# Weaving the samples' window attention into the latent stage, with another order of the recurrence levels

## The chip, the cores and the metric

The kernel runs on one core of a Trainium2 chip (trn2). The metric is the device time of one launch in microseconds (us). The kernel before takes 1953.93 us, the median of three runs (1951.99 to 1957.06).

## The reference

One inference step of a decoder trunk of two layers. A prompt of 256 tokens and eight samples of one token each (264 columns, `NT`) go through it together. A layer is

```
x += 1/2 * SwiGLU_1(RMSNorm(x))
x += W_out [ A | B | C | D ](RMSNorm(x) @ W_in)
x += 1/2 * SwiGLU_2(RMSNorm(x))
A: latent attention; for a sample over 16 pages of 128 cached latents, which are
   multiplied by w_uk and normalised before the scores, then softmax and context
B: causal dilated window attention, patterns (128,1), (512,4), (2048,16); for a sample
   the keys and values come from cache_swa_k / cache_swa_v by stride: 3 x 128 rows of 256
C: mLSTM matrix memory            D: HGRN2 gated linear recurrence, chunkwise
```

For the samples, C and D are one step of a stored state. All is float32.

## The kernel before, in words

Activations stay in SBUF, transposed (`x_T`, `h_T`: 128 x 8 x 264). All weights stream through a ring of three slots (`ring`) by DMAs that SP issues. TensorE, VectorE, ScalarE, GpSimd (called PE, DVE, ACT and POOL in the rows) and SP each run a list written out by hand, joined by semaphores. The order of work on an engine is thus the order of the calls in its loop over the layers, and an instruction that waits holds up all that stands behind it on its engine. A layer has these stages:

1. Feed-forward 1.
2. **Mixing**: the projection by `W_in` in 34 pieces (`project` on TensorE, `copy_out` on ScalarE, through two PSUM banks), and between the pieces the prompt's parts of A, B, C and D. D is computed in eight `level`s of block size 128 to 1. For a level GpSimd subtracts decays (`level_decays`, into `D1v`), ScalarE takes exponentials (`level_exp`, into `E1v`), VectorE multiplies (`level`), TensorE makes the scores (`level`), and VectorE masks them into `ATD` (`level_mask`). `hgrn` on TensorE multiplies them by the values, turns the gates of the samples and the end keys and makes the end state. Then `HCD` is normalised and turned into `o_T`.
3. **Latent stage** (`latent_samples`, on all engines): for each of the eight samples 16 pages, in pairs. TensorE turns and multiplies pages, ScalarE squares and copies, VectorE sums. A sample's scores need a maximum over all partitions. VectorE leaves `latent_max` in the next sample's time, GpSimd computes `partition_all_reduce`, and VectorE takes it up in `latent_shift` one sample later still. Between these reductions GpSimd also updates the stored states of C and D (`state_d_decay`, `state_d_products`, `state_c_decay`, `state_c_products`, after samples 2, 3, 4 and 5).
4. **Tail**: TensorE's `samples` spreads the queries over the partitions, VectorE's `states` finishes C and D, and `windows` does B: for each sample a tile of keys (`KB`, two slots, loaded by SP) is multiplied by the query (`Qbc`) and summed. Then come a maximum on GpSimd, exponentials, a sum, probabilities, the product with the values (`VB`, loaded by GpSimd's queue after the last context) and the addition into `o_T` (`mixer_done`).
5. `w_out`, then feed-forward 2.

In `latent_samples`, `b` is the sample, `g` the page and `c` a group of four pages. `settled` only moves a semaphore on.

## Time and profile before

| | |
|---|---|
| median of 3 runs | 1953.93 us |
| the profiled execution's own time | 1961.99 us |
| its span | 1960.4 us |
| TensorE matmuls busy | 1677.5 us (86%) |
| VectorE busy | 769.1 us (39%) |
| ScalarE busy | 325.7 us (17%) |
| GpSimd busy | 235.5 us (12%) |
| mean granted TensorE clock | 0.913 of full speed |

The 1.6 us between span and time lie around the program. Times in the rows count from the start of the span. In the first layer mixing runs from 270 to 515 us, the latent stage from 515 to 662, the tail from 662 to 709, `w_out` to 740. The second layer repeats this some 967 us later. In a row of the timeline the bracket tells how long the engine had been idle and what ended that; "issue" means that nothing the profile shows did. The share of busy time says little here: both feed-forward parts keep TensorE full, and the time that can go lies in the three stages between them.

### The profile page before, as it was taken

The numbers are of one execution on the slowest core, as the hardware profiler recorded it, in microseconds if no ns is written. First come the engines' busy times: TensorE is split into PE (matmuls) and PEld (weight loads), VectorE is DVE, ScalarE is ACT, GpSimd is POOL, SyncE is SP. The second block draws the span as 40 slices with busy tenths as digits, with TensorE's granted clock in tenths as the row PEclk, the third lists the DMA queues.
The fourth block names the chain that finished last, engine by engine and source line by source line (L and its number), as shares of the span: only waits on it lengthen the run. The fifth ranks groups of instructions, "written<-read, shape, count | busy, mean of one in ns | idle before, by whom it ended". The sixth has DMA issues, their size and how long they took to land.

```text
span 1960.4 us, 25417 instructions
## 1 busy us (share of the span) xinstructions
PE 1677.5 (86%) x8942; PEld 1354.5 (69%) x8942; DVE 769.1 (39%) x1403; ACT 325.7 (17%) x854; POOL 235.5 (12%) x307
## 2 busy tenths in 40 slices
PE   4999989976878368999979999899767863799998
PEld 3888867655666157888858888576665651688887
DVE  3444114653456343442124431175434645334411
ACT  1000002421545100000000000033224531000000
POOL 2000001222312310000000000012222322100000
PEclk9999999987789579999989999999777985899999
DMA  6875533320701437786548855232124024568742
GB/s 211 300 255 189 148 107 122 98 66 7 222 2 33 154 110 232 245 291 169 165 154 272 274 161 153 86 126 70 47 93 137 2 87 129 161 203 275 256 129 81
DMA packets 232153, 295.15 MB, mean 151 GB/s; under 512 B 10264, under 2 KB 215240, under 8 KB 228328
## 3 DMA queue, kind: packets, MB, share of 16 engines
q1 hardware_dynamic: 221128, 191.63, 32.2%
q0 software_dynamic: 10912, 102.08, 15.2%
q8 instruction: 62, 1.02, 0.2%
q14 instruction: 51, 0.42, 0.1%
HBM read 287.43 MB, written 73.33 MB: 184 GB/s over the span
## 4 chain that ended last, share of the span: by engine, by line
PE 75%; issue 10%; DVE 5%; POOL 2%; POOLq 2%; DVEq 1%; ACT 1%; DMA 1%; SPq 0%; ACTq 0%
PE bank L1632 32%; PE bank L1649 16%; PE bank L1670 8%; PE bank L1994 3%; PE bank L1676 3%; PE bank L1824 2%; POOLq L604 2%; PE bank L1606 2%; PE bank L1930 2%; DMA h_T<-in_cache_swa_k 1%; PE bank L1666 1%; DVE h_T L1044 1%; PE bank L1949 1%; PE bank L1872 1%; PE bank L1975 1%
## 5 line engine op out<-in xcount | busy, mean ns | idle before, releaser
L1632 PE MATMUL bank<-h_T,ring 128*128 128x264 f32 x2816 | 636.0, 390 | 27.9 <-DVE h_T L1044 27.9
L1632 PEld LDWEIGHTS bank<-h_T,ring 128*128 128x128 f32 x2816 | 540.6, 192 | 123.7 <-issue 29.9
L1649 PE MATMUL bank<-act_T,ring 128*128 128x264 f32 x1408 | 313.9, 386 | 0.0
L1649 PEld LDWEIGHTS bank<-act_T,ring 128*128 128x128 f32 x1408 | 267.5, 190 | 45.8
L1670 PE MATMUL bank<-ring,h_T 128*128 128x256 f32 (+2 forms) x512 | 162.9, 476 | 9.2 <-DVE h_T L1044 9.2
L1051 DVE TENSOR_SCALAR sg<-sg 128x264 f32<-128x264 f32 x88 | 26.2, 298 | 363.8 <-ACT sg L683 363.8
L1053 DVE RECIPROCAL sg<-sg 128x264 f32<-128x264 f32 x88 | 158.6, 1803 | 6.5
L1930 PE MATMUL bank<-wuk,TM 128*128 128x288 f32 x512 | 148.5, 437 | 0.0
L1670 PEld LDWEIGHTS bank<-ring,h_T 128*128 128x128 f32 x512 | 102.2, 204 | 62.1 <-issue 52.6
L1064 DVE SCALAR_TENSOR_TENSOR x_T<-bank,x_T 128x264 f32<-128x264 f32 x48 | 20.7, 432 | 301.3 <-PE bank L1649 259.4
L683 ACT ACTIVATE sg<-bank 128x264 f32<-128x264 f32 x88 | 34.3, 390 | 627.3 <-PE bank L1632 627.3
L1412 DVE TENSOR_REDUCE decs<-TM 128x8 f32<-128x512 f32 x128 | 87.3, 685 | 89.9 <-ACT TM L949 88.2
L1930 PEld LDWEIGHTS bank<-wuk,TM 128*128 128x128 f32 x512 | 99.4, 205 | 27.1 <-issue 2.6
L457 POOL DMA_DIRECT2D out_s_swa_k<-in_cache_swa_k x16 | 8.0, 498 | 685.0 <-DVE act_T L1057 685.0
L949 ACT ACTIVATE TM<-bank 128x512 f32<-128x512 f32 x128 | 76.4, 598 | 79.6 <-PE bank L1930 63.7
L1824 PE MATMUL bank<-ring 128*128 128x128 f32 x224 | 44.1, 377 | 49.8 <-DVE ring L1335 39.8
L1824 PEld LDWEIGHTS bank<-ring 128*128 128x128 f32 x224 | 40.5, 280 | 53.8 <-issue 53.8
L536 POOL TENSOR_TENSOR act_T<-act_T 128x256 f32<-128x256 f32 x64 | 51.5, 834 | 192.9 <-ACT act_T L832 168.2
L1994 PE MATMUL bank<-o_T,ring 128*128 128x264 f32 x256 | 60.9, 402 | 2.0 <-DVE o_T L1548 2.0
L1994 PEld LDWEIGHTS bank<-o_T,ring 128*128 128x128 f32 x256 | 50.8, 199 | 11.7 <-issue 2.4
L1676 PE MATMUL bank<-h_T,ring 128*128 128x264 f32 x256 | 58.6, 388 | 0.0
L662 ACT ACTIVATE rstd<-bank,eps 128x264 f32<-128x264 f32 x6 | 2.9, 480 | 332.6 <-PE bank L1618 332.6
(390 smaller groups left out, 1488.9 us busy)
## 6 DMA issues: line engine op xcount, KB each, us to landing
ring<-in_w_gate SPq DMA_DIRECT2D x44, 1024.0 KB, 7.3
ring<-in_w_up SPq DMA_DIRECT2D x44, 1024.0 KB, 9.6
ring<-in_w_down SPq DMA_DIRECT2D x64, 704.0 KB, 6.4
out_s_swa_k<-in_cache_swa_k POOLq DMA_DIRECT2D x16, 2047.0 KB, 10.0
out_s_swa_v<-in_cache_swa_v POOLq DMA_DIRECT2D x16, 2047.0 KB, 15.2
ring<-in_w_in SPq DMA_DIRECT2D x16, 1024.0 KB, 6.3
ring<-in_w_in SPq DMA_DIRECT2D x16, 512.0 KB, 4.4
ring<-in_w_out SPq DMA_DIRECT2D x8, 768.0 KB, 5.5
```

The source lines that it names most:

```text
L536: last = pool.tensor_tensor(dv, fv, rep(fv[:, :, mid], 2, 2 * half), SUB)
L604: pool.drain()
L949: act.activation(SQ[:, g % 4:g % 4 + 2, :], page_pairs[g // 2 % 2][:, :, 0:GW], ACT.Square)\
L1053: dve.reciprocal(sg[:, q, :], sg[:, q, :])
L1412: dve.tensor_reduce(ssq[:, b % 2, g * H:g * H + 2 * H], SQ[:, g % 4:g % 4 + 2, :].rearrange("p k (h d) -> p (k h) d", h=H), AX.X, ADD).the ...
L1632: last = pe.matmul(bank(2 * q + g, P, NT), w[:, g, c, q * P:(q + 1) * P], h_T[:, c, :], start=(c == 0), stop=(c == KC - 1))
L1649: last = pe.matmul(bank(4 + m % 2, P, NT), w[:, c, :], act_T[:, c, :], start=(c == 0), stop=(c == FT - 1))
L1670: last = pe.matmul(tile[0:ROWS[i], 0:cols], h_T[:, c, i * P:i * P + ROWS[i]], W[:, c, 0:cols], start=(c == 0), stop=(c == KC - 1))
L1676: last = pe.matmul(tile[:, 0:NT], W[:, c, i * P:(i + 1) * P], h_T[:, c, :], start=(c == 0), stop=(c == KC - 1))
L1824: last = pe.matmul(bank(bk, P, 2, 2, P)[:, h % 2, b, :], KP[:, h, b * P:(b + 1) * P], QP[:, h, b * P:(b + 1) * P], start=True, stop=True)
L1930: pe.matmul(bank(4 + g % 4, P, GW + DEC * H), latT[:, g, :], wuk[:, :], start=True, stop=True)\
L1994: last = pe.matmul(bank(4 + m % 2, P, NT), w[:, c, (m - m0) * P:(m - m0 + 1) * P], o_T[:, c, :], start=(c == 0), stop=(c == KC - 1))
```

## The change

- **Levels.** `D1v` becomes two buffers (the second in `U`, where the window scores' pairs have been read), so GpSimd may work one level ahead. On all engines the levels come earlier and lie closer together. `hgrn` is cut into parts, and the last projection pieces (`S_DG`) stand between its products and the turning of the end keys. On ScalarE `query_gates` stands ahead of `copy_out` of the values of B.
- **Queries and keys.** `spread` runs ahead of the latent stage. TensorE spreads the queries during sample 1, ScalarE copies them. SP loads keys from then on.
- **Products on GpSimd.** `window_product` multiplies a key tile in place, after the reduction of sample 1 (tile 0), 2 (1), 3 (2, 3), 4 (4) and 5 (5, 6, 7). VectorE sums them in `window_scores` in the time of samples 3 to 7. The stored states are updated one sample earlier.
- **Tail woven in.** What was `states`, `windows` and `samples` is cut up and stands between the last two samples' values and contexts.
- **Values by SP.** SP loads them behind the keys, and two of the three slabs of `W_out` stand between them, the third behind them.

```diff
@@ SP @@
-                for i, (m, k) in enumerate(OUT_SLABS):
-                    if i < RING - 1:
-                        sp.wait_ge(sem("ctx_out"), l * DEC + (2 * i + 4))
-                    else:
-                        sp.wait_ge(sem("kr_turned"), l * DEC + (KR_RING[-1] + 1))
-                    halves(w_out, m * P, k * P, FFN_SLABS + len(SLABS) + i)
...
+                    window_rows(keys, KB[:, b % K_SLOTS], b, k_loaded[b % K_SLOTS])
+                sp.wait_ge(sem("ctx_out"), l * DEC + 4)
+                for b in range(2):
+                    window_rows(vals, VB(b), b, sem("window_v_loaded"))
+                out_slab(0)
+                sp.wait_ge(sem("kr_turned"), l * DEC + (KR_RING[-1] + 1))
+                out_slab(2)
+                sp.wait_ge(sem("window_products"), (l + 1) * DEC)
+                for b in range(2, 6):
+                    window_rows(vals, VB(b), b, sem("window_v_loaded"))
+                sp.wait_ge(sem("states_summed"), l + 1)
+                for b in range(6, DEC):
+                    window_rows(vals, VB(b), b, sem("window_v_loaded"))
+                sp.wait_ge(sem("ctx_out"), l * DEC + 6)
+                out_slab(1)
@@ GpSimd @@
+            def window_product(l, b):
+                if b == 0:
+                    pool.wait_ge(sem("q_spread_copied"), l * 5 + 4)
+                    settled(pool)
+                pool.wait_ge(k_loaded[b % K_SLOTS], (l * (DEC // K_SLOTS) + (b // K_SLOTS + 1)) * 16 * NPAT)
+                settled(pool)
+                pool.tensor_tensor(KB[:, b % K_SLOTS], KB[:, b % K_SLOTS], rep(Qbc[:, b, :], 1, NPAT), MUL)\
+                    .then_inc(sem("window_multiplied"), 1)
...
-                    if i:
-                        pool.wait_ge(sem("level_exp"), l * len(LEVELS) + i)
+                    if i > 1:
+                        pool.wait_ge(sem("level_exp"), l * len(LEVELS) + (i - 1))
...
+                    if b == 1:
+                        state_d_decay(l)
                     if b == 2:
-                        state_d_decay(l)
+                        state_d_products(l)
...
+                    for i in {1: (0,), 2: (1,), 3: (2, 3), 4: (4,), 5: (5, 6, 7)}.get(b, ()):
+                        window_product(l, i)
+                    if b == 6:
+                        pool.drain()
+                        pool.wait_ge(sem("window_max"), l + 1)
...
-                pool.wait_ge(sem("ctx_done"), (l + 1) * DEC)
-                cache = t["cache_swa_v"][bass.ds(l, 1)].rearrange("a b t w -> (a b) t w")
@@ VectorE, in and behind the loop over the samples @@
+                        if g == 8:
+                            for i in {3: (0,), 4: (1,), 5: (2, 3), 6: (4,), 7: (5, 6, 7)}.get(b, ()):
+                                window_scores(l, i)
+                        if g == 10 and b == DEC - 1:
+                            window_max(l)
...
                 latent_scores(l, DEC - 1)
+                window_shift(l)
                 context(l, DEC - 3)
                 latent_sum(l, DEC - 2)
+                window_sum(l)
                 take_values(l, DEC - 2)
+                latent_shift(l, DEC - 1)
+                state_heads(l)
                 context(l, DEC - 2)
-                latent_shift(l, DEC - 1)
                 latent_sum(l, DEC - 1)
+                window_probs(l)
+                state_gates(l)
                 take_values(l, DEC - 1)
+                window_values(l)
                 context(l, DEC - 1)
+                window_heads(l)
+            def window_scores(l, b):
+                dve.wait_ge(sem("window_multiplied"), l * DEC + (b + 1))
+                dve.tensor_reduce(SB[:, b], KB[:, b % K_SLOTS].rearrange("p i (h d) -> p i h d", h=H), AX.X, ADD)\
+                    .then_inc(sem("window_products"), 1)
@@ TensorE, the loop over the layers @@
-                memory_heads(l)
-                level(l, 6)
-                project(l, tk(S_DG, 0), tk(S_DG, 1))
-                level(l, 7)
-                project(l, tk(S_DG, 1), tk(S_DG, 2))
                 hgrn(l)
+                turn_sample_gates(l)
+                project(l, tk(S_DG, 0), tk(S_DG, 2))
+                turn_end(l)
+                end_state(l)
                 latent_samples(l)
-                samples(l)
                 w_out(l)
```

On TensorE, at the end of mixing, L1666 and L1670 (L1738 and L1742 in the changed kernel) are projection pieces, L1824 (L1896) a level, L1835 to L1838 (L1907 to L1910) the products of the recurrence. Before:

```order
L1824 MATMUL bank<-ring 128x128 [waits level_taken]
L1824 MATMUL bank<-ring 128x128 x7
L1660 ISA
L1666 MATMUL bank<-ring,h_T 8x64 [waits w_in_copied]
L1666 MATMUL bank<-ring,h_T 8x64 x31
L1829 REGISTER_ALU
L1835 MATMUL bank<-TM,ring 128x64 [waits levels_done]
L1835 MATMUL bank<-TM,ring 128x64 x3
```

And in the changed kernel:

```order
L1742 MATMUL bank<-ring,h_T 128x256 [waits w_in_copied]
L1742 MATMUL bank<-ring,h_T 128x256 x7
L1901 REGISTER_ALU
L1907 MATMUL bank<-TM,ring 128x64 [waits levels_done]
...
L1678 MATMUL bank<-cst,act_T 8x128 x11
L1732 ISA
L1742 MATMUL bank<-ring,h_T 128x256 [waits w_in_copied]
L1742 MATMUL bank<-ring,h_T 128x256 x7
```

The last level has moved ahead of four projection pieces, and two pieces now stand behind the products of the recurrence and the turned gates.

On GpSimd, from the reduction (`lmx<-lmx`) of sample 4 on. Before, the state of C is updated after sample 5, and the loads of the values stand behind sample 7:

```order
L607 ISA lmx<-lmx 128x4
L490 REGISTER_ALU
L493 ISA [waits state_d_summed]
...
L499 TENSOR_TENSOR act_T<-act_T,jq 128x1024
L605 ISA
L607 ISA [waits latent_max]
L607 ISA lmx<-lmx 128x4
L605 ISA
L607 ISA lmx<-lmx 128x4 [waits latent_max]
L617 ISA
L621 ISA [waits ctx_done]
```

In the changed kernel, from the last product of the state of C (after sample 4) on:

```order
L514 TENSOR_TENSOR act_T<-act_T,jq 128x1024
L521 ISA
L523 TENSOR_TENSOR h_T<-h_T,U 128x768 [waits window_k_loaded_0]
L630 ISA
L632 ISA [waits latent_max]
L632 ISA lmx<-lmx 128x4
...
L523 TENSOR_TENSOR h_T<-h_T,U 128x768 [waits window_k_loaded_1]
L630 ISA
L632 ISA [waits latent_max]
L632 ISA lmx<-lmx 128x4
L645 REGISTER_ALU
L647 ISA wmx<-wmx 128x32 [waits window_max]
```

Three products (`h_T<-h_T,U`) now stand between the reductions of samples 5 and 6, where nothing but a reduction stood behind the state's products, and the maximum of the windows comes ahead of the reduction of sample 7.

On SP, behind the state loads. Before:

```order
L379 ISA [waits ctx_out]
L379 DMA ring<-in_w_out 128x4x384
...
L379 ISA [waits kr_turned]
L379 DMA ring<-in_w_out 128x4x256
...
L421 ISA [waits q_spread]
L421 DMA h_T<-in_cache_swa_k 128x256
```

In the changed kernel, behind the load of the seventh key tile:

```order
L415 ISA [waits window_products]
L415 DMA h_T<-in_cache_swa_k 128x256
...
L415 ISA [waits ctx_out]
L415 DMA U<-in_cache_swa_v 128x256
...
L383 DMA ring<-in_w_out 128x4x384
...
L383 DMA ring<-in_w_out 128x4x256
...
L415 ISA [waits states_summed]
L415 DMA act_T<-in_cache_swa_v 128x256
```

No value and no slab of `W_out` can be issued before the last key tile has been.

## Rows read from the trace of the kernel before

**Rows 1.** The view by windows: per engine busy us (instructions), PEclk granted clock, DMA share, GB/s.

```profile
420.00:440.00 20.00, 13.35 (x48) 10.45 (x49) 8.88 (x23) 3.52 (x9) 6.48 (x8) 0.66 0.32 104
674.00:680.00 6.00, 0.28 (x2) 0.18 (x2) 3.51 (x9) 1.76 (x10) 2.77 (x6) 0.50 0.94 295
```

**Rows 2.** Who TensorE waited for, 270 to 515 us: in total, times, longest.

```profile
PE bank L1824 <- DVE ring L1335: 19.9, 6, 5.7
...
PE bank L1824 <- DVE ring L1338: 5.0, 1, 5.0
...
PE bank L1835 <- DVE lbt L1342: 3.3, 1, 3.3
```

**Rows 3.** TensorE's timeline in mixing: start, us, engine, line, operation, operands, count [idle <-releaser].

```profile
397.75 2.05 PE L1824 MATMUL bank<-ring 128*128 128x128 f32 x16 [2.12 <-DVE ring L1335]
...
428.39 6.18 PE L1670 MATMUL bank<-ring,h_T 128*128 128x256 f32 x16
...
456.88 3.83 PE L1670 MATMUL bank<-ring,h_T 128*128 128x256 f32 x16
...
470.10 3.78 PE L1824 MATMUL bank<-ring 128*128 128x128 f32 x16 [5.69 <-DVE ring L1335]
...
486.36 1.84 PE L1666 MATMUL bank<-ring,h_T 128*8 128x64 f32 x64
...
496.63 2.77 PE L1606 MATMUL bank<-cst,act_T 128*8 128x128 f32 x12
...
514.87 4.11 PE L1930 MATMUL bank<-wuk,TM 128*128 128x288 f32 x8
```

**Rows 4.** ScalarE's timeline at the memory weights and the last level.

```profile
434.88 1.49 ACT L817 ACTIVATE U<-U 128x1536 f32<-128x1536 f32 x1
...
477.94 1.06 ACT L834 ACTIVATE act_T<-act_T 128x1024 f32<-128x1024 f32 x1
```

**Rows 5.** VectorE's timeline at the last level.

```profile
480.16 1.22 DVE L1337 TENSOR_TENSOR ring<-act_T 128x1024 f32<-128x1024 f32 x1 [4.79 <-ACT act_T L836]
```

**Rows 6.** GpSimd's timeline in the latent stage.

```profile
550.50 0.37 POOL L607 PARTITION_ALL_REDUCE lmx<-lmx  x1 [1.65 <-DVE lmx L1391]
564.30 0.37 POOL L607 PARTITION_ALL_REDUCE lmx<-lmx  x1 [13.43 <-DVE lmx L1391]
572.25 3.61 POOL L468 TENSOR_TENSOR act_T<-jq,U 128x2048 f32<-128x2048 f32 x1 [7.57 <-issue]
575.83 3.61 POOL L469 TENSOR_TENSOR act_T<-act_T,jq 128x2048 f32<-128x2048 f32 x1
586.48 0.39 POOL L607 PARTITION_ALL_REDUCE lmx<-lmx  x1 [7.04 <-issue]
...
638.37 2.34 POOL L496 TENSOR_TENSOR act_T<-act_T 128x1024 f32<-128x1024 f32 x1
...
649.30 0.39 POOL L607 PARTITION_ALL_REDUCE lmx<-lmx  x1 [6.37 <-issue]
```

**Rows 7.** VectorE's timeline during the second multiplication of the stored state.

```profile
575.95 3.51 DVE L1400 TENSOR_TENSOR decs<-nsA,lmx 128x4 f32<-128x4 f32 x1
```

**Rows 8.** Part 5 of the page: the subtraction of decays on GpSimd.

```profile
L536 POOL TENSOR_TENSOR act_T<-act_T 128x256 f32<-128x256 f32 x64 | 51.5, 834 | 192.9 <-ACT act_T L832 168.2
```

**Rows 9.** VectorE's timeline behind the last context.

```profile
661.71 2.27 DVE L1470 TENSOR_TENSOR h_T<-TM,cst 8x2048 f32<-8x2048 f32 x1
```

**Rows 10.** TensorE's timeline in the tail.

```profile
701.51 5.20 PE L1975 MATMUL bank<-U,SB 128*4 128x256 f32 x48 [1.22 <-DVE SB L1537]
...
709.16 6.18 PE L1994 MATMUL bank<-o_T,ring 128*128 128x264 f32 x19 [0.98 <-DVE o_T L1548]
```

**Rows 11.** The view of DMAs: what, issuer, count, KB each, median us to landing.

```profile
h_T<-in_cache_swa_k SPq DMA_DIRECT2D x48, 128.0 KB, 2.3
```

**Rows 12.** SP's timeline at the state loads.

```profile
515.34 0.35 SPq L401 DMA_DIRECT2D U<-scratch  x1
515.89 0.33 SPq L401 DMA_DIRECT2D act_T<-in_state_mlstm_C  x1
```

More of the change, by code:

```diff
@@ L829, in level_exp @@
                 if half > 1:
-                    dv, ev = (v.rearrange("p h (n r s) -> p (h n) r s", r=2, s=half) for v in (D1v, E1v))
+                    dv, ev = (v.rearrange("p h (n r s) -> p (h n) r s", r=2, s=half) for v in (D1v[i % 2], E1v))
                     act.activation(ev[:, :, 0, :], dv[:, :, 0, :], ACT.Exp, scale=-1.0)
@@ L859, in _ @@
                 copy_up(l)
+                query_gates(l)
                 copy_out(l, tk(S_BV, 0), tk(S_BV, 1))
@@ L982, in _ @@
                 last.then_inc(sem("states_copied"), 1)
-                act.wait_ge(sem("window_shifted_max"), l + 1)
-                act.activation(SB[:, :, :, :], SB[:, :, :, :], ACT.Exp, scale=B_SCALE)
-                act.activation(wmx[:, 3, :], wmx[:, 3, :], ACT.Exp, scale=B_SCALE).then_inc(sem("window_exp"), 1)
+                act.wait_ge(sem("oA_out"), l + 1)
+                for i in range(2):
+                    last = act.copy(o_T[:, i, :], bank(4 + i, P, NT))
+                last.then_inc(sem("oA_copied"), 1)
                 norm(l, 2)
@@ new lines, in spread_new, with state_sums @@
+            def spread_new(l):
+                s = slice(0, DEC)
+                pe.wait_ge(sem("q_spread_copied"), l * 5 + 4)
+                pe.matmul(bank(3, P, DEC, H), ones[s, 0:P], nsm[:, 1], start=True, stop=True)
+                for g in range(2):
+                    last = turn(cut(ps[3], DEC * H, 2, DEC)[:, g, :], TM[s, 2, BV + g * P:BV + (g + 1) * P], DEC)
+                last.then_inc(sem("vnew_turned"), 1)
+            def state_sums(l):
+                pe.wait_ge(sem("page_taken"), (l + 1) * (DEC * PAGES))
+                pe.wait_ge(sem("states_summed"), l + 1)
+                pe.matmul(bank(5, 32, 2 * HD + 1), cst[:, K_SELJ:K_SELJ + 32], red[:, :], start=True, stop=True)\
+                    .then_inc(sem("red_out"), 1)
@@ new lines, in window_sums, with turn_states @@
+            def window_sums(l):
+                pe.wait_ge(sem("window_summed"), l + 1)
+                pe.matmul(bank(6, P, DEC * H), ones[:, 0:P], wmx[:, 4, :], start=True, stop=True).then_inc(sem("window_sum_out"), 1)
+            def turn_states(l):
+                pe.wait_ge(sem("heads_ready"), l + 1)
+                settled(pe)
+                for g in range(2):
+                    last = turn(bank(4 + g, HD, 32), HS[:, g, :], 32)
+                last.then_inc(sem("states_turned"), 1)
@@ new lines, in window_values @@
+            def window_values(l):
+                pe.wait_ge(sem("window_v_loaded"), (l + 1) * DEC * NPAT * 16)
+                pe.wait_ge(sem("window_probs"), l + 1)
+                pe.wait_ge(sem("window_cleared"), l + 1)
+                for r in range(DEC // QUADS):
+                    for i in range(NPAT):
+                        for j in range(QUADS):
+                            b = QUADS * r + j
+                            last = pe.matmul(bank(7, P, 2, GW)[32 * j:32 * j + H, r, :], SB[:, b, i, :], VB(b)[:, i, :],
+                                             start=(i == 0), stop=(i == NPAT - 1))
+                last.then_inc(sem("window_out"), 1)
@@ L1884, in latent_samples, with turn_window @@
+            def turn_window(l):
+                pe.wait_ge(sem("window_taken"), l + 1)
+                for g in range(2):
+                    for r in range(DEC // QUADS):
+                        last = turn(bank(0, P, 2, 2, P)[:, g, r, :], Vs[:, r, g, :], P)
+                last.then_inc(sem("window_turned"), 1)
             def latent_samples(l):
@@ L2019, in _ @@
                 turn_qk(l)
+                level(l, 0)
                 project(l, tk(S_MQK, 2), tk(S_MV, 0))
-                level(l, 0)
+                level(l, 1)
                 turn_qk_sample(l)
```

304 lines of the change are left out of this document (152 added, 152 removed).

## The prediction

> **What bounds the kernel now.** I read the windows first, then who TensorE waited for, then the timelines of the engines it waits for. In the feed-forward parts TensorE is full and the change leaves them alone. Three stretches of a layer are not full.
>
> Mixing: TensorE waits for VectorE's level products for 19.9 + 5.0 us and for the last mask for 3.3 us [rows 2]. The pauses also cost clock: from 420 to 440 us the granted clock is 0.66 [rows 1], a mean of the two levels 2.4 and 1.2 GHz. A level takes 2.05 us before and 3.78 after a wait of 5.69 us, and a piece 6.18 instead of 3.83 [rows 3].
>
> Latent stage: GpSimd sets its length. When a tensor operation follows a reduction, GpSimd starts it 7.57 us later with nothing to wait for; when a reduction follows a tensor operation, it starts 7.04 or 6.37 us later; a reduction behind a reduction has only the wait for VectorE [rows 6]. I read this as a switch between two kinds of code, some 14 us for the way there and back. The reductions of samples 2 and 6 end at 564.67 and 649.69 [rows 6]: four such visits in 85.0 us, each longer than the 13.8 us that sample 1 to 2 took (550.87 to 564.67), which is the pace of the pages.
>
> Tail: from the end of sample 6's reduction to the first matmul of `w_out` at 709.16 [rows 10] pass 59.5 us. Of these 12.0 are the last two samples' values and contexts, up to 661.71 [rows 9]. The other 47.4 are the tail, in which TensorE's only long work is the product with the values, 5.20 us [rows 10].
>
> **The levels.** Removed: the 25.0 us of waits at the levels and 3.3 at the last mask, 28.3 us per layer [rows 2]. A second `D1v` lets GpSimd subtract while ScalarE's exponential of the level before is pending, and on all engines each level now has a piece (3.83 us [rows 3]) between it and the next, about the time of a mask and a product. I went through the five lists in the new order with the durations of the same instructions. What stays or comes:
> - 2.4 us, because ScalarE copies the values of B only behind `query_gates`, and the turn of the first probabilities waits for what stands behind that copy. All of it is on TensorE's path, which is full there.
> - 2.3 and 0.6 us at levels 3 and 4, behind the softmax shift and `memory_inputs` on VectorE.
> - 5.3 us at level 7: behind the memory weights ScalarE has 1.49 us and two small exponentials, then twice 1.06 us for the level [rows 4], then VectorE twice 1.22 us [rows 5]. TensorE has only `memory_scores`, about 2 us, to cover it.
> - 3.5 us at the end. The products of the recurrence and the turned gates (until 499.4 [rows 3]) now stand ahead of the last pieces, so they no longer follow the last piece (which ends at 488.2). But the sigmoid and products of the last output gate, the normalising and the turn do. I count 19.0 us from the last piece to the first page, against 15.5 from 499.4 to 514.87 [rows 3].
>
> The clock gives back between nothing and 9.2 us: four levels at about 1.7 us too much and one piece at 2.35. I take 4, since a wait of 5.3 us stays. Sum: 28.3 - 2.4 - 2.9 - 5.3 - 3.5 + 4.0 = 18.2 us per layer; bounds 9 (each level still waits 1 us more, no clock) and 23.4 (all of the clock). GpSimd's gathers and stores follow the last piece and the end keys as before, so the first reduction moves with the first page.
>
> **The latent stage.** The queries' spread costs TensorE about 8 us during sample 1, where it waits for the first reduction anyway in this trace; ScalarE's copies too. I cost them at nothing; without that cover they cost 8. The state update moves up one sample without a change of length. Added on GpSimd: a fifth visit (the samples' reductions 1 and 2 no longer follow each other), and eight products. A product of 128x768 is not in the trace. By 3.61 us for 128x2048 [rows 6] it costs 1.35 us, by 2.34 for 128x1024, with all operands read in full [rows 6], 1.76, by 834 ns for 128x256 [rows 8], 2.50. I take 1.76, the row nearest in form, and 0.2 for its semaphores: 16 us for eight (12 to 22). Tile 7 waits for a slot that VectorE frees only in sample 7. The tile lands 2.3 us after issue [rows 11] and SP needs about 0.55 us for each of three issues [rows 12]: 4 us, of which tile 6's product covers one, so 3.3. Reductions 1 to 6 then take 85.0 + 14.0 + 16 + 3.3 = 118.3 us instead of 98.8: **19.5 us more**.
>
> Which engine should multiply is a matter of the page too. The Trainium skill (GPSIMD Engine Reference, "3.1 Elementwise — side-by-side cycle accounting") says that elementwise work belongs on VectorE, since an addition of 2048 float32 takes 4497 ns on GpSimd and 2293 on VectorE. An estimate from that page gives 1.7 us for a product, or 13.5 for eight where I have 14 without semaphores. By its rule the products are on the wrong engine, and here they lie on the engine that sets the stage's length.
>
> VectorE's eight sums (under 1 us each) and its waits for a product lie beside GpSimd's visits. Tiles 1, 4 and 7 are waited for longest, tile 1 about 13 us. The sums of the pages, and so ScalarE and TensorE, are queued behind that wait. They have a GpSimd visit's time to catch up.
>
> **The tail.** Removed: 59.5 us from reduction 6 to `w_out`. In its place, from the same point: shift and scores 1.9; window shift 1.3; context and sum 1.2; values 2.0 and their copy 0.4; shift, state heads and context of the last two samples 3.7; last exponential and sum 0.4; window probabilities and gates 1.8; turn and last values 2.3; product with the values 5.2 [rows 10]; the last sum and context 1.9 (its copy lies beside); the latent heads' matmuls and ScalarE's copies 2.8; a semaphore 0.2. Together **25.1 us**, so 34.4 less. What hides the rest is GpSimd's visits.
>
> This holds if the values are there 15 us after reduction 6. SP issues tile 7, 24 value tiles and two slabs in the 27.5 us before that, 6.2 MB: 224 GB/s are needed. From 674 to 680 us the trace shows 295 [rows 1], which makes 21 us; 31 issues of 0.55 us make 17. The third slab comes well before its turn.
>
> Latent stage and tail: 34.4 - 19.5 = 14.9 us per layer; bounds 4 (products at 22, some 5 of the spread uncovered) and 19 (products at 12).
>
> **Sum.** 18.2 + 14.9 = 33.1 us per layer, 66.2 for two. The profiled execution took 1961.99 us (span 1960.4), so the profile should be near 1896; against the median, 8.06 lower, 1953.93 - 66.2 = **1888 us**. All costs at their good ends give 1869, at their bad ones 1928.
>
> **Rivals.**
> - *The levels give nothing.* The waits move to other instructions, above all ScalarE's list, where copies and exponentials stand in one row. For it: two of my four kept waits are ScalarE's. Against: it is busy 3.52 of 20 us there [rows 1]. Then 1954 - 2 x 14.9 = 1924 with no gain, 1906 with half.
> - *The values come late.* SP can't issue one before tile 7, and key tiles of 3 x 128 KB in 2.3 us [rows 11] are only 171 GB/s. At that rate 6.2 MB take 36 us, 8.7 more per layer: 1905.
> - *VectorE is locked out.* While GpSimd multiplied from 575.83 on, a VectorE operation on 128x4 took 3.51 us [rows 7], to the end of GpSimd's. Each product then also costs VectorE up to 1.8 us, which matters only on its critical half sample: about 3 x 1.8 per layer, 1899. The Trainium skill (GPSIMD Engine Reference, "8. Key points") names the shared SBUF interfaces and VectorE's instructions with two SBUF inputs; the row agrees.
> - *Slower: the two engines wait for each other.* Product i is summed in the middle of a sample, and the scores that the next reduction but one needs come half a sample of pages (9 us), a state sum and 1.5 us later, 14 us together. GpSimd's visit in between lasts 23. Each visit grows from the point where that half sample takes more than some 23 us. To eat 33 us per layer over five visits it must take 30, twice what I count: 1960 and more. Only a TensorE at 1.2 GHz throughout, with VectorE locked out, would do that.
>
> **Chances.** My case (1869 to 1900) 0.58, levels at half or nothing 0.20, values late or VectorE locked out (to 1910) 0.12, better than all my good ends 0.06, slower 0.04. Leaving out about a fifth, the range is 1866 to 1920. A measurement of this kernel can tell about 0.3% (6 us): faster 0.95, same 0.01, slower 0.04.
>
> **What would show it.** In the profile of the changed kernel: TensorE's waits for the level products down from 24.9 to about 8 us, the longest at level 7; first page near 497 us instead of 514.87; five visits of GpSimd with both switches around each, 22 to 25 us apart, and a product of 1.8 us; reduction 6 118 us behind reduction 1; `w_out` 25 us behind reduction 6, with TensorE's product with the values waiting for probabilities and not for a DMA. I am wrong if the reductions lie more than 26 us apart, if the values' DMA ends last, or if mixing keeps its length.

## The result and the profile after

The changed kernel takes **1884.49 us** (median, 1881.82 to 1889.51) against 1952.96 (1951.65 to 1957.06) before: ratio 0.9649, 95% interval 0.9623 to 0.9675, 68.5 us less. The prediction was 1888 us. The profiled execution took 1883.08 us, its span 1881.5 (before 1960.4). The two spans differ by 78.9 us, the medians by 68.5, since the profiled execution of the kernel before lies 9.0 us above its median and that of the changed kernel 1.4 below. What is read from this pair of traces below is thus to be held against the 78.9, 39.4 per layer.

The windows from 270 us to the first page, before (first line) and after; columns as in [rows 1]:

```profile
270.00:514.80 244.80, 202.15 (x1380) 151.55 (x1378) 113.08 (x189) 67.75 (x159) 50.60 (x66) 0.88 0.24 78
```

```profile
270.00:490.30 220.30, 191.77 (x1373) 141.59 (x1371) 114.92 (x192) 68.01 (x159) 51.25 (x66) 0.90 0.26 86
```

The first page comes at 490.30 us instead of 514.87, 24.6 us sooner. TensorE's busy time for the same work falls by 10.4 us (202.15 to 191.77), which is clock but for about 1 us of 7 records that are missing after, and its idle time by 14.1 (42.65 to 28.53, each window less TensorE's busy time). The stretch that answers to [rows 1], and the one with the values' transfers:

```profile
420.00:440.00 20.00, 20.00 (x178) 18.03 (x178) 13.39 (x31) 6.00 (x15) 5.41 (x7) 0.91 0.22 67
638.00:649.00 11.00, 1.58 (x6) 1.11 (x6) 3.24 (x6) 1.26 (x4) 0.81 (x1) 0.50 1.01 321
```

The clock is 0.91 where it was 0.66. The waits that answer to [rows 2], here from 270 to 500 us:

```profile
PE bank L1678 <- DVE U L1404: 8.7, 1, 8.7
PE bank L1896 <- DVE ring L1376: 5.0, 1, 5.0
...
PE bank L1896 <- DVE ring L1373: 3.7, 3, 2.2
PE bank L1678 <- ACT U L776: 2.4, 1, 2.4
```

Level products are waited for 8.7 us instead of 24.9. TensorE's timeline, against [rows 3]: an undisturbed level, level 7, and the first page behind the last turn:

```profile
398.51 2.05 PE L1896 MATMUL bank<-ring 128*128 128x128 f32 x16
...
447.23 3.78 PE L1896 MATMUL bank<-ring 128*128 128x128 f32 x16 [4.97 <-DVE ring L1376]
...
486.00 1.97 PE L1678 MATMUL bank<-cst,U 128*128 128x128 f32 x8 [8.72 <-DVE U L1404]
...
490.30 3.27 PE L2065 MATMUL bank<-wuk,TM 128*128 128x288 f32 x8
```

GpSimd's timeline in the latent stage, against [rows 6]:

```profile
526.72 0.37 POOL L632 PARTITION_ALL_REDUCE lmx<-lmx  x1 [1.66 <-DVE lmx L1434]
534.56 3.61 POOL L483 TENSOR_TENSOR act_T<-jq,U 128x2048 f32<-128x2048 f32 x1 [7.47 <-issue]
...
541.72 1.79 POOL L523 TENSOR_TENSOR h_T<-h_T,U 128x768 f32<-128x768 f32 x1
550.52 0.39 POOL L632 PARTITION_ALL_REDUCE lmx<-lmx  x1 [7.02 <-issue]
...
575.27 0.39 POOL L632 PARTITION_ALL_REDUCE lmx<-lmx  x1 [6.50 <-issue]
587.36 0.26 POOL L498 TENSOR_SCALAR jq<-jq,sst 128x16 f32<-128x16 f32 x1 [11.70 <-issue]
...
600.80 0.39 POOL L632 PARTITION_ALL_REDUCE lmx<-lmx  x1 [6.49 <-issue]
...
623.32 0.39 POOL L632 PARTITION_ALL_REDUCE lmx<-lmx  x1 [6.54 <-issue]
630.67 3.58 POOL L523 TENSOR_TENSOR h_T<-h_T,U 128x768 f32<-128x768 f32 x2 [6.97 <-issue]
637.00 1.80 POOL L523 TENSOR_TENSOR h_T<-h_T,U 128x768 f32<-128x768 f32 x1 [2.76 <-DMA h_T<-in_cache_swa_k]
649.96 0.39 POOL L632 PARTITION_ALL_REDUCE lmx<-lmx  x1 [11.16 <-issue]
650.70 0.54 POOL L647 PARTITION_ALL_REDUCE wmx<-wmx  x1 [0.35 <-issue]
```

Call the stretch from one reduction over tensor operations to the next reduction a visit; there are five. Ahead of the first tensor operation of a visit and ahead of the reduction that ends it stand 6.5 to 7.8 us of "issue". Twice it is longer, 11.70 us ahead of the decay of C and 11.16 ahead of reduction 6. Reductions 1 and 6 end at 527.09 and 650.35: 123.3 us, where 98.8 was before. The last two reductions lie 26.6 us apart. The tail, against [rows 10], on TensorE:

```profile
654.00 1.89 PE L1954 MATMUL bank<-U,decs 128*4 128x128 f32 x32 [10.79 <-DVE mxs L1449]
...
661.29 0.28 PE L1678 MATMUL bank<-cst,HS 32*64 32x32 f32 x2 [3.98 <-DVE HS L1561]
...
668.45 0.66 PE L1678 MATMUL bank<-cst,act_T 128*128 128x128 f32 x4 [0.29 <-DVE act_T L1608]
...
671.34 8.94 PE L2101 MATMUL bank<-o_T,ring 128*128 128x264 f32 x39 [1.04 <-ACT o_T L1023]
```

`w_out` starts 21.0 us behind reduction 6 (before 59.5), and TensorE waits for no DMA. Its waits are for VectorE's sums and heads. Reduction 1 to `w_out` takes 144.3 us instead of 158.3, and `w_out` stands at 671.34 instead of 709.16, 37.8 us sooner. From the first page to reduction 1 it is 0.8 us longer than before (36.8 against 36.0). `w_out` itself is 1.6 us shorter (28.4 us from its first matmul to the start of its last, before 30.0): before, its first 19 matmuls took 6.18 us [rows 10], now its first 39 take 8.94. So at the end of its `w_out` the first layer is 39.4 us ahead, half the difference of the spans. In layer 2 reductions 1 to 6 take 125.3 us.

### The profile page after: what moved, and what is told of

Same layout as the page of the kernel before. It is cut to its first block, busy times and chain, and to the rows that moved or that the text cites. A ratio compares the mean times of both kernels' runs of the same rounds, so it can differ in the third digit from the quotient of the medians.

```text
span 1881.5 us, 25437 instructions
## 1 busy us (share of the span) xinstructions
PE 1653.3 (88%) x8942; PEld 1334.9 (71%) x8942; DVE 752.1 (40%) x1387; ACT 326.1 (17%) x854; POOL 239.6 (13%) x275
## 4 chain that ended last, share of the span: by engine, by line
PE 73%; issue 10%; DVE 5%; POOL 3%; ACT 2%; DVEq 2%; POOLq 2%; DMA 1%; SPq 0%; ACTq 0%
PE bank L1704 34%; PE bank L1721 17%; PE bank L1742 7%; PE bank L2101 3%; PE bank L2065 2%; PE bank L1748 2%; PE bank L1896 2%; POOLq L629 2%; PE bank L1678 1%; PE bank L1738 1%; DVE h_T L1082 1%; PE bank L1954 1%; POOL h_T L523 1%; DMA h_T<-in_cache_swa_k 0%; DVE bsum L1413 0%
## 5 line engine op out<-in xcount | busy, mean ns | idle before, releaser
L1704 PEld LDWEIGHTS bank<-h_T,ring 128*128 128x128 f32 x2816 | 541.2, 192 | 123.5 <-issue 29.8
L1742 PE MATMUL bank<-ring,h_T 128*128 128x256 f32 (+2 forms) x512 | 163.2, 476 | 9.2 <-DVE h_T L1082 9.2
L1091 DVE RECIPROCAL sg<-sg 128x264 f32<-128x264 f32 x88 | 158.7, 1803 | 6.5
L2065 PE MATMUL bank<-wuk,TM 128*128 128x288 f32 x512 | 155.0, 451 | 0.0
L1742 PEld LDWEIGHTS bank<-ring,h_T 128*128 128x128 f32 x512 | 101.6, 203 | 61.4 <-issue 53.0
L2065 PEld LDWEIGHTS bank<-wuk,TM 128*128 128x128 f32 x512 | 103.4, 213 | 29.0 <-issue 2.6
L1748 PEld LDWEIGHTS bank<-h_T,ring 128*128 128x128 f32 x256 | 48.2, 190 | 9.0 <-issue 1.1
L1678 PE MATMUL bank<-cst,U 128*128 128x128 f32 (+2 forms) x200 | 33.2, 307 | 23.2 <-DVE U L1404 17.5
L1963 PE MATMUL bank<-cst,TM 128*128 128x4 f32 x32 | 7.2, 295 | 49.9 <-DVE TM L1423 49.9
```

The costliest lines, as they stand in the source:

```text
L1091: dve.reciprocal(sg[:, q, :], sg[:, q, :])
L1678: return pe.transpose(out, src, ident[0:rows, 0:rows])
L1704: last = pe.matmul(bank(2 * q + g, P, NT), w[:, g, c, q * P:(q + 1) * P], h_T[:, c, :], start=(c == 0), stop=(c == KC - 1))
L1742: last = pe.matmul(tile[0:ROWS[i], 0:cols], h_T[:, c, i * P:i * P + ROWS[i]], W[:, c, 0:cols], start=(c == 0), stop=(c == KC - 1))
L1748: last = pe.matmul(tile[:, 0:NT], W[:, c, i * P:(i + 1) * P], h_T[:, c, :], start=(c == 0), stop=(c == KC - 1))
L2065: pe.matmul(bank(4 + g % 4, P, GW + DEC * H), latT[:, g, :], wuk[:, :], start=True, stop=True)\
```

## The experiments

The theory: three terms make the gain. The new order closes the levels' gaps and keeps the clock up; GpSimd sets the latent stage by a switch between reductions and tensor operations, some 14 us per visit; the woven tail is hidden behind it. The rivals are named in each expectation. All times are medians, and each ratio is against the kernel before as measured beside that version. Its median was 1957.37 us beside one_more_switch, exp_early, vector_products and two_visits, 1954.69 beside old_order, one_buffer, values_after and gathers_split, 1962.51 beside quiet_queue and 1952.96 beside the changed kernel. So a difference of two versions from different sets is uncertain by some 5 us, and where it matters it is given by the ratios too.

**one_more_switch: the price of a visit.**

```diff
+                    if b == 0:
+                        pool.tensor_tensor(wmx[:, 2, 0:1], ones[:, 0:1], ones[:, 0:1], MUL)
                     if b == 1:
                         state_d_decay(l)
```

> The changed kernel with one tensor operation more on GpSimd, a product of 128x1 into wmx (which the window's reduction overwrites later), right behind the reduction of sample 0. The operation itself is under 0.3 us. Theory (GpSimd's change between reductions and tensor operations costs some 14 us for the way there and back, and GpSimd sets the length of the latent stage): reduction 1, which now comes 2.4 us behind reduction 0, comes 14 us behind it; all later reductions and w_out move by the same 12 to 14 us per layer, so 24 to 28 us in all: near 1884.5 + 26 = 1910. Rival 1 (the time around a visit is the wait for data or for VectorE, not a switch): the small operation costs its own time, 1884 to 1886. Rival 2 (there is a switch, but the pages' pace sets the stage): reduction 1 is late, reduction 6 is not, under 1888.

1907.41 us, ratio 0.9732 (0.9703 to 0.9761), 22.9 us over the changed kernel by the medians and 16 by the two ratios, less than the 24 to 28 expected. GpSimd's timeline of this run:

```profile
525.93 0.39 POOL L632 PARTITION_ALL_REDUCE lmx<-lmx  x1 [27.75 <-issue]
533.61 0.18 POOL L634 TENSOR_TENSOR wmx<-ones 128x1 f32<-128x1 f32 x1 [7.29 <-issue]
540.05 0.39 POOL L632 PARTITION_ALL_REDUCE lmx<-lmx  x1 [6.26 <-issue]
547.94 3.61 POOL L483 TENSOR_TENSOR act_T<-jq,U 128x2048 f32<-128x2048 f32 x1 [7.50 <-issue]
```

An operation of 0.18 us moves reduction 1 from 2.0 to 14.1 us behind reduction 0, and `w_out` from 671.3 to 685.1 in layer 1, 26.7 us in all by the last matmul of `w_out` in layer 2. Rivals 1 and 2 fall: the gap comes with the change of operation and not with data, and it is on the path.

**exp_early: why visit 3 starts late.**

```diff
-                    if b == 3:
+                    if b == 2:
                         act.wait_ge(sem("state_m"), l + 1)
                         act.activation(sst[:, 7:10], sst[:, 4:7], ACT.Exp).then_inc(sem("state_exp"), 1)
```

> The changed kernel with the exponential of the memory's state decay (state_exp on ScalarE) issued one sample earlier, behind the latent exponential of sample 2 instead of sample 3. In the trace of the changed kernel it runs at 579.72 us, and GpSimd's decay of C starts at 587.36, 11.70 us behind reduction 3, where other visits start 7.0 to 7.8 us behind theirs. Theory (GpSimd starts to switch only when the awaited exponential is there, and the change moved the state update up by a sample without it): the gap falls to 7.5 us, reductions 3 to 4 lie 21.4 us apart instead of 25.5, 4 us per layer, 8 in all: 1876 to 1878. Rival (the gap is the switch itself, slowed by something else, or the 4 us turn up again as a wait of VectorE's page sums): the distance from reduction 1 to reduction 6 stays 123 us and the time within 0.3% of 1884.5.

1871.96 us, ratio 0.9551 (0.9526 to 0.9576): 12.5 us less by the medians, 19 by the ratios, 10.2 by the spans of the two profiled runs, and `w_out` starts 4.3 us earlier in layer 1; 8 were expected. GpSimd's timeline:

```profile
573.90 0.39 POOL L632 PARTITION_ALL_REDUCE lmx<-lmx  x1 [6.55 <-issue]
581.60 0.26 POOL L498 TENSOR_SCALAR jq<-jq,sst 128x16 f32<-128x16 f32 x1 [7.31 <-issue]
...
595.33 0.39 POOL L632 PARTITION_ALL_REDUCE lmx<-lmx  x1 [6.77 <-issue]
```

The gap is 7.31 us instead of 11.70, and reductions 3 and 4 lie 21.4 us apart instead of 25.5. In the changed kernel ScalarE runs the exponential only behind reduction 3:

```profile
579.72 0.20 ACT L976 ACTIVATE sst<-sst 128x3 f32<-128x3 f32 x1
```

The decay starts 7.4 us behind its end, about a whole switch: the switch begins only when the awaited value is there.

**values_after and quiet_queue: why the last way back takes 11 us.**

```diff
 values_after
-                sp.wait_ge(sem("window_products"), (l + 1) * DEC)
+                sp.wait_ge(sem("window_max_all"), l + 1)
                 for b in range(2, 6):
 quiet_queue
-                sp.wait_ge(sem("ctx_out"), l * DEC + 4)
+                sp.wait_ge(sem("window_max_all"), l + 1)
                 for b in range(2):
```

> The changed kernel with SP loading the value tiles of samples 2 and on only behind the reduction of the window's maxima, instead of behind the sum of key tile 7. In the changed kernel these loads and two slabs of w_out run at 323 GB/s from 638 to 650 us, and in just this time GpSimd takes 11.16 us from the last product to reduction 6, where its other ways back take 6.4 to 7.2; around those the trace has one instruction packet of some 10 KB on a DMA queue. Theory (the way back loads code by DMA, and the transfers in front of it delay it): with the queues empty the gap is 6.5 to 7 us, reduction 6 comes 4.5 us earlier behind the last product; but the values then land later, some 20 us behind the reduction, so that TensorE's product with the values waits for a DMA and w_out moves by 3 to 10 us: 1884 to 1900 in all. Rival (the gap is long because three products, a DMA wait or something else stands before it): it stays 11 us.

> The changed kernel with SP waiting for the reduction of the window's maxima before it issues any value tile or slab of w_out. In the run with only the values of samples 2 and on held back, the first two value sets and two slabs still moved 3.0 MB at 231 GB/s between the last product and reduction 6, and GpSimd's way back took 11.54 us as in the changed kernel (11.16). Here nothing but key tile 7 is under way. Theory (traffic on the DMA queues delays GpSimd's way back): the gap is 6.4 to 7.2 us. Rival (the gap belongs to the visit itself, three products with a wait for a DMA between them): it stays 11 to 12 us. In both cases values and slabs come late: 6.2 MB at some 300 GB/s is 21 us, TensorE waits for them for 8 to 15 us per layer, 1895 to 1915 in all.

values_after: 1896.29 us, ratio 0.9699 (0.9678 to 0.9721); the gap stayed 11.54 us, but the values of two samples and two slabs still kept the DMA engines busy, so the run did not tell the theories apart. quiet_queue: 1906.51 us from two runs, ratio 0.9733 (0.9645 to 0.982), so its time is only roughly known; the readings below are of its trace. Its windows and GpSimd's timeline:

```profile
633.00:640.00 7.00, 1.58 (x6) 1.11 (x6) 3.24 (x6) 1.26 (x4) 1.41 (x1) 0.50 0.00 0
```

```profile
626.02 3.57 POOL L523 TENSOR_TENSOR h_T<-h_T,U 128x768 f32<-128x768 f32 x2 [7.04 <-issue]
632.61 1.80 POOL L523 TENSOR_TENSOR h_T<-h_T,U 128x768 f32<-128x768 f32 x1 [3.02 <-DMA h_T<-in_cache_swa_k]
640.61 0.39 POOL L632 PARTITION_ALL_REDUCE lmx<-lmx  x1 [6.19 <-issue]
```

With nothing else under way the way back takes 6.19 us (6.24 in layer 2), in the same visit with its three products and its wait for tile 7. In the changed kernel reduction 6 doesn't wait for VectorE either: its input is complete at 627.15, before the products. So having the values and slabs in flight costs this way back 5 us. It isn't the rate alone that does it. In vector_products (below) slabs and values are loaded beside a way back too, at 257 GB/s over the gap, and it takes 7.04 us:

```profile
588.95:595.99 7.04, 3.18 (x18) 2.37 (x16) 1.37 (x2) 3.08 (x11) 0.00 (x2) 1.00 0.88 257
```

```profile
595.99 0.38 POOL L632 PARTITION_ALL_REDUCE lmx<-lmx  x1 [7.04 <-issue]
```

In values_after it was 253 GB/s over the gap and 11.54 us. Whether it is how much is queued, or when in the gap it moves, that makes the difference isn't shown.

The price of the late values, from TensorE's waits in quiet_queue, 620 to 700 us (in total, times, longest):

```profile
PE bank L2008 <- DMA act_T<-in_cache_swa_v: 16.1, 1, 16.1
```

In values_after this wait is 7.2 us. The changed kernel has none. Of the three places that were tried for its loads this one is the fastest, and the 5 us are its price.

**old_order: the two halves of the change.** The lists of ScalarE, VectorE and TensorE from the queries' bound to the first page are in the order of before; both `D1v` are kept. TensorE's part, for levels 1 to 4:

```diff
-                level(l, 1)
                 turn_qk_sample(l)
 ...
-                level(l, 2)
-                project(l, tk(S_MV, 2), tk(S_MV, 3))
-                level(l, 3)
-                project(l, tk(S_MV, 3), tk(S_MV, 4))
+                level(l, 1)
+                project(l, tk(S_MV, 3), tk(S_DI, 0))
                 turn_probs(l, 1)
-                project(l, tk(S_MV, 4), tk(S_DI, 0))
-                level(l, 4)
+                level(l, 2)
```

> The changed kernel with the lists of all engines in the order of the kernel before, from the queries' bound to the first page (levels, projections, copies, gates); both D1v buffers and all of the woven window attention stay. It prices the new order alone: old_order less the changed kernel; and the kernel before less old_order is the weave. Theory (the order of the levels gives 24.6 us per layer by the first page of the two traces, 514.87 against 490.30, and the weave the rest, 13 to 14 us): 1884.5 + 49 = 1933, TensorE's waits for the level products 20 to 25 us per layer again, the first page near 513, the time from the first page to w_out as in the changed kernel, 181 us. Rival (the second D1v alone gives a good part, since GpSimd's difference no longer waits for ScalarE): 1900 to 1920. Rival 2 (the weave gives more and the levels less, because the stage behind absorbs part of an early first page): under 1915.

1931.13 us, ratio 0.9882 (0.9862 to 0.9902). The order is worth 46.6 us (45.5 by the two ratios), 23.3 per layer; the weave, against the kernel before, 23.1 us (19 to 27), 11.6 per layer. TensorE's waits, 270 to 520 us:

```profile
PE bank L1899 <- DVE ring L1376: 19.2, 6, 5.0
...
PE bank L1899 <- DVE ring L1379: 5.0, 1, 5.0
```

The levels' products are waited for 24.2 us, as before, and the first page is at 513.9 us. Both rivals fall.

**one_buffer: what the second buffer is worth.**

```diff
-        D1v = [cut(actf, 4 * H * NT, H, SEQ), cut(U, 2048, H, SEQ)]
+        D1v = [cut(actf, 4 * H * NT, H, SEQ)] * 2
 ...
-                    if i > 1:
-                        pool.wait_ge(sem("level_exp"), l * len(LEVELS) + (i - 1))
+                    if i:
+                        pool.wait_ge(sem("level_exp"), l * len(LEVELS) + i)
```

> The changed kernel with one D1v buffer, as before: GpSimd subtracts for a level only when ScalarE's exponential of the level before has been issued. The order stays new. Theory (in the new order the levels lie close, and each needs its difference ready when ScalarE comes to it; GpSimd's difference takes 1 to 2 us and would now stand in the chain of each level where ScalarE comes at once): waits of TensorE grow by 0 to 2 us at three to five levels, 3 to 8 us per layer: 1890 to 1900. Rival (a piece of 3.8 us lies between two levels, so GpSimd has the time anyway): within 0.3% of 1884.5, first page within 1 us of 490.3.

1883.76 us, ratio 0.9636 (0.9611 to 0.9661): the same time. The theory fell; the rival was right. A piece between two levels gives GpSimd all the time it needs.

**vector_products and two_visits: fewer visits.**

```diff
 both, in window_scores (VectorE); GpSimd's window_product goes
-                dve.wait_ge(sem("window_multiplied"), l * DEC + (b + 1))
+                slot = KB[:, b % K_SLOTS]
+                dve.wait_ge(k_loaded[b % K_SLOTS], (l * (DEC // K_SLOTS) + (b // K_SLOTS + 1)) * 16 * NPAT)
+                dve.tensor_tensor(slot, slot, rep(Qbc[:, b, :], 1, NPAT), MUL)
+                dve.drain()
 two_visits too, on GpSimd
                     if b == 1:
                         state_d_decay(l)
-                    if b == 2:
                         state_d_products(l)
                     if b == 3:
                         state_c_decay(l)
-                    if b == 4:
                         state_c_products(l)
```

Both also sum two tiles in each of the samples 3 to 6. two_visits moves `state_exp` to sample 1 as well, and VectorE's first sum of the state from sample 4 to 3.

> The changed kernel with the window's products on VectorE: it multiplies each key tile in place and sums it (tiles 0 and 1 in sample 3, 2 and 3 in sample 4, and so on), GpSimd has the four state visits alone, so its fifth visit and all its products go. Theory (GpSimd's switches and products set the stage): visits of 22.0, 22.6, 21.7 and 20.3 us less the products of 1.8, 1.8, 3.6 and 1.8 us, 20.2 + 20.8 + 18.1 + 18.5 = 77.6 us from reduction 1 to 5, then 2 us to reduction 6 and a sample's pages, some 12 us, to reduction 7; w_out 19.5 us behind that. Reduction 1 to w_out 111 us instead of 144, less 4 to 9 us that VectorE's eight extra products (0.9 us each) and the pages may take back: 24 to 33 us per layer, 1820 to 1836. Rival 1 (VectorE is what the pages wait for, so 8 products of about 1 us and its own tile waits cost as much as they save): 1870 to 1885. Rival 2 (values set the end once the rest is shorter): TensorE's product with the values waits for a DMA, 1840 to 1860.

> As the kernel with the products on VectorE, and the state update in two visits of GpSimd instead of four: decay and products of D behind reduction 1, of C behind reduction 3, with state_exp behind the exponential of sample 1. Theory (each visit costs a switch pair of 14 us): visit 1 is 7.4 + 15.6 + 6.5 = 29.5 us, visit 3 is 7.5 + 10.5 + 6.5 = 24.5, the reductions behind them 2 us apart, then 12 to 14 us per sample by the pace of the pages: reduction 1 to 7 84 us, and w_out 19.5 behind it: 103 us instead of 144, 41 per layer, 1800 to 1815. Rival (the pages' pace, with VectorE's products in it, sets the stage already with four visits): the same as the kernel with four visits, within 10 us.

vector_products: **1838.39 us**, ratio 0.9387 (0.936 to 0.9413). Just outside the expected range. Reduction 1 to 5 took 93.0 us, not 77.6. I had taken the visits of the changed kernel too short (they are 23.8, 24.8, 25.5 and 22.5 us, 87.6 in all without the products), and the state's exponential, queued behind VectorE's and ScalarE's work for sample 5, runs at 578.02, so the decay of C starts 14.04 us behind reduction 3. two_visits: **1811.55 us**, ratio 0.9253 (0.9227 to 0.928), as expected. It saves 27 us on vector_products, so its rival falls. Not all of that is the merging: with the exponential moved up, the gap ahead of the decay of C is 7.33 us instead of 14.04, which may be up to 6.7 us per layer, and the two parts weren't run apart. GpSimd's timeline of two_visits:

```profile
524.73 0.37 POOL L632 PARTITION_ALL_REDUCE lmx<-lmx  x1 [1.65 <-DVE lmx L1430]
532.57 3.61 POOL L483 TENSOR_TENSOR act_T<-jq,U 128x2048 f32<-128x2048 f32 x1 [7.47 <-issue]
...
554.49 0.39 POOL L632 PARTITION_ALL_REDUCE lmx<-lmx  x1 [6.33 <-issue]
562.39 0.37 POOL L632 PARTITION_ALL_REDUCE lmx<-lmx  x1 [7.52 <-DVE lmx L1430]
570.09 0.26 POOL L498 TENSOR_SCALAR jq<-jq,sst 128x16 f32<-128x16 f32 x1 [7.33 <-issue]
...
587.04 0.39 POOL L632 PARTITION_ALL_REDUCE lmx<-lmx  x1 [6.36 <-issue]
593.05 0.37 POOL L632 PARTITION_ALL_REDUCE lmx<-lmx  x1 [5.62 <-DVE lmx L1430]
606.70 0.37 POOL L632 PARTITION_ALL_REDUCE lmx<-lmx  x1 [13.29 <-DVE lmx L1430]
...
615.59 0.38 POOL L632 PARTITION_ALL_REDUCE lmx<-lmx  x1 [4.18 <-DVE lmx L1430]
```

Two visits of 30 and 25 us, and from 587 on GpSimd waits for VectorE's scores, at the pace of the pages. Reductions 1 to 6 take 82.0 us. It and gathers_split are the fastest versions, 73 us under the changed kernel by the medians.

**gathers_split: the first reduction.** Built on two_visits.

```diff
-                for b in range(4, DEC):
+                for b in range(4, 6):
                     gather_latents(b)
-                gather_rotary(DEC - 1)
 ...
+                    if b == 2:
+                        for i in range(6, DEC):
+                            gather_latents(i)
+                        gather_rotary(DEC - 1)
```

> As two_visits, with the gathers of the latents of samples 6 and 7 and of the last rotary keys issued behind reduction 2 instead of ahead of reduction 0. In two_visits reduction 0 ends at 523.1, 27.4 us behind the last gather's issue, and VectorE and TensorE wait for it for 3 to 4 us. Theory (GpSimd's drain ahead of the first reduction waits until its gathers have landed, the last about 19 us behind its issue, and then comes the way to the reductions' code): with 2 MB less in the queue reduction 0 comes 4 to 7 us earlier, TensorE's wait of 3.1 us goes; reduction 3 had 7.5 us of slack, in which three gathers of 1.3 us fit: 1803 to 1810. Rival (a gather is other code than a reduction, or the drain ahead of reduction 3 waits for the landing too): reduction 3 comes 5 to 15 us later, 1815 to 1835.

1810.84 us, ratio 0.9257 (0.9236 to 0.9277): no change. Reduction 0 starts at 512.44 instead of 522.69, so the gathers do hold it up, but reduction 1 comes at 522.83 instead of 524.73, because it waits for the pages, and reduction 3 at 565.38 instead of 562.39, behind the moved gathers. 1803 to 1810 was expected, 1815 to 1835 by the rival, and it is neither: each was right for one reduction, and they cancel. Whether it is the landing or the issue of the gathers that the drain waits for isn't separated.

## Why the prediction was right, step by step

The sum was 33.1 us per layer; by the medians it was 34.2, by the two traces 39.4. Three terms were off by 4 to 6 us each: two gains were larger than predicted, one loss too. That 1888 lies so near 1884.49 is thus partly luck. The errors cancel in part, and the rows came from an execution 9 us above its median: the prediction put the profiled execution near 1896, and it took 1883.08.

| step | predicted | measured |
|---|---|---|
| levels: waits gone, net of what stays | 14.2 | 14.1 (idle time of TensorE) |
| levels: clock | 4.0 (0 to 9.2) | 10.4, of it about 1 missing records |
| GpSimd, reductions 1 to 6 | 19.5 longer | 24.5 longer |
| reduction 6 to `w_out` | 34.4 shorter | 38.5 shorter |
| first page to reduction 1 | 0 | 0.8 longer |
| `w_out` itself | 0 | 1.6 shorter |

**The levels: right in mechanism, clock under-sized.** (The bound of 9 us comes out as 14.2 less 1 us at each of the five levels that keep no wait; at all eight, as it reads, it would be 6.2. The last range doesn't hang on it.) Each kept wait came as foretold: 2.4 us for the first probabilities (2.4), 2.3 and 0.6 at levels 3 and 4 (2.2 and 0.9), 5.3 at level 7 (5.0), 19.0 us from the last piece to the first page (18.6). old_order shows that the order makes all of it. What failed is the sentence that the clock gives back 4 us "since a wait of 5.3 us stays": TensorE's busy time fell by 10.4, above even the 9.2 of the bound. (The missing records don't explain it: old_order has 1370 records for this work, fewer than the changed kernel's 1373, and 201.26 us of busy time, 9.5 more.) I had counted only the levels and one slow piece, but [rows 1] is a mean over the whole stretch, and other matmuls behind the gaps were slow too: the turns of the samples' gates and the later products of the recurrence took 421 ns each before and take 273 to 275 now. `w_out` gained by the clock as well, a term that the sum lacks: 1.6 us. In its first 4.9 us the granted clock is 1.00 where it was 0.65. A second step was needless: the second `D1v`, which I named as the first cause of the closed gaps, has no effect (one_buffer).

**GpSimd's chain: right in mechanism, 5 us short.** By one of the prediction's own signs it is wrong here: reductions were to lie at most 26 us apart, and the last two lie 26.6 us apart in layer 1, in layer 2 27.4, and reductions 3 and 4 27.1. The causes are the two below. As foretold, there are five visits with both switches, a product of 1.79 to 1.81 us (1.76 taken), tile 7 waited for 2.8 us (3.3 taken). Two things were missed. The wait for `state_exp`: the prediction says that the state update moves up one sample without a change of length, and did not follow its exponential, which stayed behind sample 3 in ScalarE's list. It costs 4.1 us by exp_early. And the last way back, 11.16 instead of 6.4 us, beside the transfers that the prediction counted for their bandwidth alone. It costs 5.0 us by quiet_queue. The products and their semaphores were 1.6 us cheaper than taken and the wait for tile 7 0.5, which leaves 2 us that came shorter and that I can't place.

GpSimd starts an operation mostly 6.2 to 8.2 us behind a change between reductions and tensor operations, and nothing in the profile fills the time. The Trainium skill (GPSIMD Engine Reference, "2.1 Instruction dispatch") says that the first call of freshly loaded code pays a load of about 6 us that no instruction of the profile shows. In quiet_queue the way back with the DMA engines idle is of about that length (6.19 us); the way there takes mostly 7 to 8 us where nothing is awaited. That the gap is this load, and that transfers slow it, is inferred; what is shown is the gap, and that one of them is 10.8 to 12.5 us with the values and slabs in flight.

**The tail: right, 4 us too long.** The order and the waits are as listed; the product with the values took 4.4 us by its rows (5.2 taken) and starts when the probabilities and the last values are there.

**The rivals.** *The levels give nothing*: they gave 23.3 us. *The values come late*: not here; issued 11 to 13 us later behind the last product, they make TensorE wait 7.2 us per layer (values_after). *The two engines wait for each other*: visits were 22.5 to 26.6 us in layer 1 and up to 27.4 in layer 2, and they didn't grow to 30. *VectorE is locked out*: it happens, with the state's operations more than with the products. VectorE's timeline while GpSimd adds (558.75 to 563.25) and multiplies (the other three rows; `latn` in the second is a scalar per partition in SBUF):

```profile
539.20 2.58 DVE L1441 TENSOR_TENSOR lmx<-lmx,nsA 128x4 f32<-128x4 f32 x1
...
558.95 4.32 DVE L1413 TENSOR_SCALAR bsum<-decs,latn 128x4 f32<-128x4 f32 x1
...
563.65 3.38 DVE L1418 TENSOR_TENSOR ctxT<-bsum 128x4 f32<-128x4 f32 x1
...
567.72 0.67 DVE L1455 TENSOR_REDUCE decs<-TM 128x8 f32<-128x512 f32 x1
```

An operation on 128x4 takes 4.32 us instead of 0.22 (the same line at 545.15), while a sum of 128x512, with one input, takes its usual 0.67 beside GpSimd's product of 566.97 to 568.78. In the changed kernel that is hidden, because all wait for GpSimd anyway. In two_visits it is on the path: TensorE waits 6.51 us at 545.04 for scores behind such an operation of 4.54 us. The Trainium skill (GPSIMD Engine Reference, "8. Key points") names VectorE's instructions with two SBUF inputs; the first and the third row agree, and the second was held with one tensor and one scalar from SBUF.

**The engine of the products.** The Trainium skill's rule that the prediction weighed (GPSIMD Engine Reference, "3.1 Elementwise — side-by-side cycle accounting"), elementwise work belongs on VectorE, is borne out: moving the products saved 46 us by the medians, 23 per layer. The reason is only in part the page's, that GpSimd is slower at them (1.80 us for a product, VectorE 0.95). What left GpSimd is 14.4 us of products and 20.9 of the fifth visit's switches and its wait for tile 7. Merging visits, with the exponential moved up, saved 27 us more.

## What to carry to other kernels

Count an engine's changes between kinds of operations before you count the operations themselves: here a visit's two switches cost 13 to 15 us whatever it held, more where an input came late or transfers were in flight, so gather the operations into few visits, and look at what the awaited input's own engine does just before. When a step is moved, move everything it waits for. And when you price a clock, go through every matmul that runs slow behind a pause, not only the slowest that you see, and also the stage that follows.

## What the runs showed of the hardware

- GpSimd's change from tensor operations back to reduction 6 took 6.19 and 6.24 us with no loads beside it (quiet_queue), and 10.8 to 12.5 us with values and slabs of `W_out` in flight at 253 to 340 GB/s over the gap (changed kernel, old_order, one_buffer, values_after, exp_early, one_more_switch, both layers). A like rate beside other ways back, 231 to 257 GB/s in vector_products and 255 in gathers_split, left them at 6.6 to 8.1 us, so the rate alone doesn't decide it.
- The change to tensor operations starts only when the awaited value is there: the decay starts 7.4 us behind the end of the exponential in the changed kernel and 7.3 in vector_products, and with the value there beforehand 7.31 us behind the reduction (exp_early).
- The first reduction behind GpSimd's gathers starts 24 to 28 us behind the end of the last gather's issue with five in front (all kernels but one), 19 us with two (gathers_split).
